# All modulation rows summed in the first stage, and expert value sums on four tiles of the TensorE array

## The chip, the cores and the metric

The kernel runs on one core of a Trainium2 chip. It is one launch that computes two networks one after the other, in float32. The metric is the device time of a launch in microseconds (us); less is better.

## The reference, cut to what matters

The first network has two layers over 256 rows of `x` and 256 rows of `ctx`, 1024 wide. Each layer begins from modulation rows, one matrix product of two vectors with a large weight:

```python
mod_x = silu(c) @ ada_w[i] + ada_b[i]        # 1024 x 6144 weights per layer
mod_c = silu(c_ctx) @ ada_w[i] + ada_b[i]
sh1, sc1, g1, sh2, sc2, g2 = split(mod_x, 6)
xn = rmsnorm(x, norm1_g[i]) * (1 + sc1) + sh1
x = x + g1 * mixer(xn)                       # layer 0: chunk mixer, layer 1: state-space mixer
x = x + g2 * peer(rmsnorm(x, norm2_g[i]) * (1 + sc2) + sh2)
```

`peer` picks, for each token and each of 8 heads, 16 of 16384 experts, and needs a row `u` and a row `v` of each:

```python
ue, ve = take(u_tab, ids), take(v_tab, ids)              # 1024 wide each
act = gelu(einsum("nd,nhkd->nhk", h, ue))
y = einsum("nhk,nhkd->nd", g * act, ve)
```

`ctx` goes through the same in layer 0, and in layer 1 only gives the state-space mixer its starting state. The second network (attention, latent attention, two feed-forwards) follows and is not touched.

## The kernel before

**Stages.** The front (0 to about 310 us) makes the modulation rows of layer 0, the chunk mixer of `ctx`, and the matrices of the state-space mixer. The first expert stage, `peer0` (about 304 to 1828 us), sums experts for 256 `ctx` tokens and then 256 `x` tokens; in its gaps run, as "fill", the chunk mixer of `x`, the modulation rows of group 0 of layer 1 (`ada1`), and the state-space input, states and scan of `ctx`. Then comes the state-space mixer of `x` (about 1828 to 2060), the second expert stage `peer1` (about 2100 to 2786), and the second network.

**Modulation rows.** A layer's weight is 24 blocks of 1 MB, in three groups of 8: group 0 holds shift and scale of the first norm, group 1 the mixer's gate and the second norm's shift, group 2 that norm's scale and the expert gate. `Rows` (L465) does one group: `load(j)` puts a block in a slot of `W`, after the slot's last user (`w_used`); `pe` sums it with 64 matmuls of 64 columns whose outputs lie on four column tiles of the array (L495); `add_bias` (L504) takes the sums and adds the bias on DVE; `store` (L513) sends four small DMAs from ACT's queue to `mod_scr`, from which the norms load them. The front holds the three groups of layer 0, two blocks between two blocks of the mixer's input product (`pe_in`, L627). `ada1` sits in the fill of `peer0`, at `ADA1_ROW`. The last two groups of layer 1 are `LateRows` (L1636 to 1664): 16 blocks loaded by POOL, pair by pair, into buffers that the first expert stage has left, and summed between the pieces of the state-space mixer of `x`.

**Expert stage.** For each of 512 or 256 (block of tokens, head, choice) triples, a "row": POOL gathers for 128 tokens the row of `u` and of `v` (1 MB, L1350) into a ring of 8; DVE multiplies with `h` and sums (L1326); ACT does gelu, the gate, and scales the identity to a 128 x 128 diagonal `DIAG` (L1218, L1220, L1223); PE multiplies the diagonal with the two halves of `v` into two banks (L1165), accumulating over 16 rows, a "unit". After a unit `add_rows` on DVE multiplies both banks by the gate (L1307, 1024 columns at once) and adds to `XA` (L1308), at the tenth row of the next unit. Between rows PE does the queries of later heads (L1126) and one step of fill. Steps of the fill are placed by row numbers.

**State-space mixer of x.** Eight chunks; each is cut by ACT from `u_scr`, turned (L1444), summed with a 1 MB matrix of `min_scr` (L1690), turned again (L1708), and copied by ACT and DVE (L1501, L1522). DVE then scans 31 steps for the first half of the groups (`dve_scan(0)`, four chunk copies inside it) and 31 for the second half; output products (L1828, L1830) follow each half, then the projection (L1873).

**Order.** Each engine's instructions are in program order, as are the DMAs of a queue. SP issues nearly all weight loads; ACT issues the stores of matrices and rows, so a slow issue there holds up its copies. The orders of the front are written out in `first_sync`, `first_pe`, `first_act`, `first_dve`, `first_pool`.

Of the kernel before, what the change touches and what calls it, by code (L numbers as in the profile page):

```python
# [15 lines left out]
ALU = mybir.AluOpType  # L16
# [9 lines left out]
P = 128  # L26
D = 1024
KT = D // P
# [76 lines left out]
def program(nc, t):  # L105
    with ExitStack() as ctx:
# [361 lines left out]
        class Rows:  # L468
# [3 lines left out]
            def __init__(self, layer, grp, slots, bank, bias, stage, saved):  # L472
                self.layer, self.grp, self.slots, self.bank = layer, grp, slots, bank
                self.bias, self.stage, self.saved = bias, stage, saved
                self.slot_of = [slots[j % len(slots)] for j in range(8)]
                self.n = [use(s) for s in self.slot_of]
                self.kept, self.stored = saved.plan(1), mod_stored.plan(64)
                bias_in.plan(16)
# [4 lines left out]
            def load_bias(self, eng):  # L483
                eng.dma_start(self.bias, t["ada_b"][self.layer * 3 + self.grp].rearrange("p (a e) -> p a e", a=2)).then_inc(bias_in.sem, 16)

            def pe(self, row0=0, per=1, blocks=range(8)):
                for j in blocks:
                    s = self.slot_of[j]
                    if j == 0:
                        pe.wait_ge(self.saved.sem, self.kept if self.saved is sums_taken else self.kept - 1)  # L490
# [10 lines left out]
            def add_bias(self):  # L501
                v.wait_ge(bias_in.sem, 64 if self.layer else 48)
# [89 lines left out]
        class Mixer:  # L592
# [60 lines left out]
            def pe_mix(self):  # L653
                yield from until("pe", self.mix_row)
                pe.wait_ge(w_full[3], (self.n_ws + 1) * 16)
                for j in range(2):
                    pe.wait_ge(v_done.sem, self.vv + j + 1)
# [377 lines left out]
        class Peer:  # L1035
# [10 lines left out]
            DIAG = view(20224, 4, P)  # L1046
# [98 lines left out]
            def pe(self, fill, after_first=None):  # L1145
# [7 lines left out]
                for r in range(self.rows):  # L1153
# [46 lines left out]
            def act(self, fill, after_first=None, tail=iter(())):  # L1200
# [9 lines left out]
                for u in range(self.units):  # L1210
                    a.wait_ge(gate_ready.sem, self.gr + u + 1)
                    for k in range(TOPK):
# [10 lines left out]
                        a.mul(self.DIAG[:, r % 4, :], IDENT, self.WGT[:, u % 2, k:k + 1]).then_inc(diag_ready.sem, 1)  # L1223
# [75 lines left out]
            def add_rows(self, u):  # L1299
# [6 lines left out]
                sums = PS[:, 4 + (u % 2) * 2:6 + (u % 2) * 2, :].rearrange("p a b -> p (a b)")  # L1306
                dve.link(v, v.tensor_tensor(self.YG, sums, gate, ALU.mult))  # L1307
# [5 lines left out]
            def dve(self, fill, tail=iter(())):  # L1313
                for u in range(2):
                    drain(self.choose(u))
                self.gates(0)
# [298 lines left out]
        STAGE2 = [AR[0:ADA_LANES, at:at + 512] for at in (23680, 24192)]  # L1615
# [4 lines left out]
        ROW_IN = [XA[:, 2:4, :].rearrange("p t d -> p (t d)"), H[:, 2:4, :].rearrange("p t d -> p (t d)"), view(14464, BLK), view(16512, BLK)]  # L1620
        BIAS2 = [HT[0:ADA_LANES, 2 * i:2 * i + 2, SEQ:SEQ + COLS] for i in range(2)]


        row_in, row_used, row_added = [sem(f"ada2_in{u}") for u in range(2)], sem("ada2_used"), sem("ada2_added")
        row_out, bias2_in = [sem(f"ada2_out{u}") for u in range(2)], sem("ada2_bias_in")

        class LateRows:


            BANK, PAIRS = 6, 8  # L1630

            def load(self, p):
                for j in (2 * p, 2 * p + 1):
                    if j >= 4:
                        g.wait_ge(row_used, p - 1)
                    g.dma_start(ROW_IN[j % 4], t["ada_w"][32 + j]).then_inc(row_in[p % 2], 16)  # L1636

            def load_bias(self):
                for grp in range(2):
                    sp.dma_start(BIAS2[grp], t["ada_b"][4 + grp].rearrange("p (a e) -> p a e", a=2)).then_inc(bias2_in, 16)  # L1640

            def pe(self, p):
                if p == 0:
# [1660 lines left out]
```

## Time and profile before

| | us |
|---|---|
| median of three runs | 3702.83 (3699.62 to 3703.74) |
| the profiled execution, time | 3701.66 |
| its span, first to last instruction | 3699.7 |
| PE, DVE, ACT, POOL busy | 3170.0, 2248.0, 1430.1, 969.0 |
| moved by DMA | 1152.69 MB, mean 312 GB/s |

Line numbers are those of the kernel before. A recorded float32 matmul is two instructions, so the two matmuls of a row show as x4. The profiled execution's time lies 1.17 us under the median, and 1.96 us of it lies outside the span.

### The profile page before, as it was taken

Reading aid. Unit: us, or ns where it says so; the run is one execution under the profiler, and the core shown is the slowest. Engines: PE = TensorE matmul, PEld = TensorE weight load, DVE = VectorE, ACT = ScalarE, POOL = GpSimd, SP = SyncE. Lnnn points to the kernel's source line nnn. Section 1 sums busy time; section 2 is a strip of 40 time slices with the busy share of each in tenths; the row PEclk is TensorE's granted clock in tenths of the full one; section 3 lists DMA queues with packets and bytes.
Section 4 is the critical chain, followed back from the end, with each engine's and each line's share of the span. In section 5 each row is a group of like instructions: output and inputs, shape, how many; then the busy total and the mean of one; then the engine's idle time right before and its main releaser. Section 6 shows DMA issues by size and latency. Waiting matters only on the chain. (4 is left out here: it accounts for less than half of the span.)

```text
span 3699.7 us, 46712 instructions
## 1 busy us (share of the span) xinstructions
PE 3170.0 (86%) x15952; PEld 2093.8 (57%) x15952; DVE 2248.0 (61%) x5034; ACT 1430.1 (39%) x3564; POOL 969.0 (26%) x796
## 2 busy tenths in 40 slices
PE   4977999899888998897767798888877989889898
PEld 3865566454434654442356644444325789777897
DVE  6855667666667666679424467666762259513397
ACT  1223443444334444443223244444432247423275
POOL 0002434434333334444200154444560000000000
PEclk8977999999999999999877899999998989999899
DMA  7748999999999999999876499999992325332353
GB/s 278 289 169 320 420 415 413 421 419 417 420 420 395 411 407 415 414 419 348 364 274 214 174 421 421 421 421 416 414 418 108 120 104 181 136 117 105 120 183 119
DMA packets 177137, 1152.69 MB, mean 312 GB/s; under 512 B 21860, under 2 KB 30264, under 8 KB 43306
## 3 DMA queue, kind: packets, MB, share of 16 engines
q0 software_dynamic: 113936, 827.38, 54.6%
q1 hardware_dynamic: 56058, 304.90, 21.9%
q10 hardware_dynamic: 6944, 17.91, 1.3%
q8 instruction: 105, 1.72, 0.2%
q14 instruction: 94, 0.77, 0.1%
HBM read 1128.86 MB, written 21.25 MB: 311 GB/s over the span
## 5 line engine op out<-in xcount | busy, mean ns | idle before, releaser
L1165 PE MATMUL PS<-AR 128*128 128x512 f32 x3072 | 1510.2, 618 | 252.0 <-ACT AR L1223 245.7
L1350 POOL DMA_INDIRECT AR<-in_peer_uv,AR x768 | 955.8, 1245 | 1503.5 <-PE PS L1165 1095.2
L1326 DVE CUSTOM_DVE_ANT_0 AR<-AR,H 128x1024 f32<-128x1024 f32 x768 | 940.7, 1225 | 655.8 <-DMA AR<-in_peer_uv,AR 637.0
L1165 PEld LDWEIGHTS PS<-AR 128*128 128x128 f32 x3072 | 558.8, 193 | 856.9 <-issue 419.0
L1218 ACT ACTIVATE SM<-SM 128x1 f32<-128x1 f32 x768 | 155.3, 202 | 1130.4 <-DVE SM L1326 1126.1
L1126 PEld LDWEIGHTS PS<-HT,W 128*128 128x128 f32 x1536 | 299.7, 195 | 271.0 <-issue 254.6
L1126 PE MATMUL PS<-HT,W 128*128 128x256 f32 x1536 | 428.1, 387 | 2.0 <-issue 1.3
L1223 ACT ACTIVATE AR<-CON,SM 128x128 f32<-128x128 f32 x768 | 308.4, 402 | 48.1 <-PE PS L1165 23.7
L2623 PE MATMUL PS<-XP,WP 128*128 128x256 f32 x2112 | 265.2, 288 | 13.2 <-ACT WP L2769 7.0
L2623 PEld LDWEIGHTS PS<-XP,WP 128*128 128x128 f32 x2112 | 264.0, 197 | 15.6 <-issue 7.3
L1220 ACT ACTIVATE SM<-SM 128x1 f32<-128x1 f32 x768 | 226.3, 295 | 25.0
L627 PE MATMUL PS<-W,HT 128*128 128x256 f32 x768 | 192.8, 391 | 5.8 <-ACT AR L724 2.8
L627 PEld LDWEIGHTS PS<-W,HT 128*128 128x128 f32 x768 | 149.5, 197 | 37.7 <-issue 16.2
L2769 ACT CAST WP<-AR 128x2048 fp32r<-128x2048 f32 x66 | 126.5, 1917 | 49.9 <-DVE AR L2612 49.9
L2815 DVE TENSOR_TENSOR WP<-W,AR 128x2048 fp32r<-128x2048 f32 x62 | 142.1, 2292 | 2.1
L2623 PE MATMUL PS<-WP,GVP 128*128 128x512 f32 x528 | 128.0, 399 | 11.8 <-DVE GVP L2618 11.8
L2623 PEld LDWEIGHTS PS<-WP,GVP 128*128 128x128 f32 x528 | 100.6, 194 | 33.1 <-issue 12.6
L2612 DVE TENSOR_SCALAR AR<-W 128x2048 uint32<-128x2048 uint32 x62 | 75.8, 1223 | 18.8 <-PE PS L2623 15.6
L495 PE MATMUL PS<-W,SM 128*2 128x64 f32 x2048 | 48.8, 241 | 36.3 <-DMA W<-in_ada_w 33.3
L495 PEld LDWEIGHTS PS<-W,SM 128*2 128x2 f32 x2048 | 34.1, 93 | 61.4 <-issue 36.2
L1242 DVE MAX8 SM<-AR 128x8 f32<-128x128 f32 x96 | 23.2, 283 | 71.3 <-ACT AR L1192 40.8
L2974 PE MATMUL PS<-HT,W 128*128 128x256 f32 x288 | 65.0, 388 | 0.5 <-ACT HT L262 0.5
(374 smaller groups left out, 3414.1 us busy)
## 6 DMA issues: line engine op xcount, KB each, us to landing
W<-in_peer_w_q SPq DMA_DIRECT2D x48, 1024.0 KB
W<-in_ada_w SPq DMA_DIRECT2D x32, 1024.0 KB
W<-in_ffn_out SPq DMA_DIRECT2D x22, 1024.0 KB
W<-in_ffn_gate SPq DMA_DIRECT2D x20, 1024.0 KB
W<-in_ffn_val SPq DMA_DIRECT2D x20, 1024.0 KB
W<-in_cm_w_in SPq DMA_DIRECT2D x16, 1024.0 KB
AR<-min_scr SPq DMA_DIRECT2D x16, 1024.0 KB, 10.3
AR<-in_peer_uv,AR POOLq DMA_INDIRECT x768
```

The costliest lines, as they stand in the source:

```text
L495: mm = pe.matmul(PS[32 * c:32 * c + 2, self.bank, j * ADA_PART:(j + 1) * ADA_PART], CS[:, k, :], W[:, s, at:at + ADA_PART], start=(k == 0) ...
L627: mm = pe.matmul(self.bank(i)[:, j * COLS:(j + 1) * COLS], HT[:, k, tb * P:(tb + 1) * P], W[:, slot, k * COLS:(k + 1) * COLS], start=(k == ...
L1126: mm = pe.matmul(PS[:, j % 2, 0:2 * P], W[:, j // 2, k * COLS + (j % 2) * P:k * COLS + (j % 2 + 1) * P], HT[:, k, first:first + 2 * P], st ...
L1165: mm = pe.matmul(PS[:, 4 + (u % 2) * 2 + c, :], self.DIAG[:, r % 4, :], self.UV[:, r % RING, D + c * 512:D + (c + 1) * 512], start=(k == 0 ...
L1218: a.activation(self.GELU[:, u % 2, one], self.ACTV[:, u % 2, one], ACT.Gelu_apprx_tanh).then_inc(gelu_done.sem, 1)
L1220: a.mul(self.WGT[:, u % 2, one], self.GELU[:, u % 2, one], self.GATE[:, u % 2, one]).then_inc(w_ready.sem, 1)
L1223: a.mul(self.DIAG[:, r % 4, :], IDENT, self.WGT[:, u % 2, k:k + 1]).then_inc(diag_ready.sem, 1)
L1326: v.tensor_tensor_reduce(rows_, rows_, H[:, self.tb(u), :], 1.0, 0.0, ALU.mult, ALU.add, self.ACTV[:, u % 2, k:k + 1]).then_inc(u_used.sem, 1)
L1350: g.indirect_dma_start(out=self.UV[:, r % RING, :], out_offset=None, in_=t["peer_uv"], in_offset=bass.IndirectOffsetOnAxis(ap=self.IDS[:, ...
L2623: mm = pe.matmul(out, lhs[i], rhs[j], start=(start and n == 0), stop=(stop and n == 2))
L2769: a.copy(WP[:, s, 0, :], WT).then_inc(high_done, 1)
L2815: v.tensor_tensor(WP[:, s, 1, :], src, WT, ALU.subtract).then_inc(split_done, 1)
```

## The change

It has two parts.

**Rows.** `ada` is now six `Rows`, all in the front; `ada1`, `LateRows` and their semaphores, waits, loads and stores are gone. The second group of layer 0 is summed whole before the mixer's first block; groups 2 and 3 go between the eight blocks of `pe_in`, one pair after each; groups 4 and 5 go, pair by pair, between the two halves of `pe_mix`, after `pe_turn`, after the sixth and the seventh piece of the matrices, and after each of the four blocks of `pe_out`. All of them use slots 0 and 1. `add_bias` and `store` of each follow on DVE and ACT. SP's load order is rewritten to match, and the peer stage's own first loads stand behind the last row block. The load of `x` now waits for all six groups (`mod_stored` 384 in place of 192).

**Value sums.** A row's two matmuls (128 x 128 diagonal, 512 columns) become four, each on a 64 x 64 tile: token half `half` is the row half of the array and picks the bank, column half `c` of `v` is the column half. The diagonal is 128 x 64 (`EYES`, two stacked 64 x 64 identities, made once per expert stage). `add_rows` takes the sums in four pieces of 64 partitions x 512 columns in place of one of 128 x 1024.

```diff
+                self.n_th, self.layer, self.grp, self.bank, self.saved = n, n // 3, n % 3, 6 + n % 2, ada_saved
+                self.slots = slots = (0, 1) if n else (0, 1, 2, 3)
 ...
-                    for c in range(2):
-                        mm = pe.matmul(PS[:, 4 + (u % 2) * 2 + c, :], self.DIAG[:, r % 4, :], self.UV[:, r % RING, D + c * 512:D + (c + 1) * 512],
-                                       start=(k == 0), stop=(k == TOPK - 1))
+                    for x in range(2):
+                        for half in range(2):
+                            c, rows_ = (half + x) % 2, slice(half * self.HP, (half + 1) * self.HP)
+                            mm = pe.matmul(PS[c * self.HP:(c + 1) * self.HP, 4 + (u % 2) * 2 + half, :], self.DIAG[rows_, r % 4, :],
+                                           self.UV[rows_, r % RING, D + c * 512:D + (c + 1) * 512], start=(k == 0), stop=(k == TOPK - 1))
 ...
-                        a.mul(self.DIAG[:, r % 4, :], IDENT, self.WGT[:, u % 2, k:k + 1]).then_inc(diag_ready.sem, 1)
+                        a.mul(self.DIAG[:, r % 4, :], self.EYES, self.WGT[:, u % 2, k:k + 1]).then_inc(diag_ready.sem, 1)
 ...
-                sums = PS[:, 4 + (u % 2) * 2:6 + (u % 2) * 2, :].rearrange("p a b -> p (a b)")
-                dve.link(v, v.tensor_tensor(self.YG, sums, gate, ALU.mult))
+                for i in range(2):
+                    for c in range(2):
+                        out, here, cols = slice(i * self.HP, (i + 1) * self.HP), slice(c * self.HP, (c + 1) * self.HP), slice(c * 512, (c + 1) * 512)
+                        one = v.tensor_tensor(self.YG[out, cols], PS[here, 4 + (u % 2) * 2 + i, :], gate[here, cols], ALU.mult)
+                dve.link(v, one)
 ...
-            for b in range(4):
+            mixc.load_out(0)
+            for one in ada[4:6]:
+                one.load_bias(sp)
+            for b in range(6):
+                ada[4].load(b)
+            for b in range(1, 4):
                 mixc.load_out(b)
+                for at in (2 * b + 4, 2 * b + 5):
+                    ada[4 + at // 8].load(at % 8)
+            for b in range(4, 8):
+                ada[5].load(b)
             peer0.sync(fill_sync())
 ...
             for b in range(8):
                 drain(mixc.pe_in(b))
-                if b < 7:
-                    at = (2 * b + 2) % 8
-                    drain(ada0[1 if b < 3 else 2].pe(blocks=range(at, at + 2)))
+                at = 2 * b % 8
+                drain(ada[2 + b // 4].pe(blocks=range(at, at + 2)))
                 if b in (1, 2, 4, 5, 7):
                     prep.pe((1, 2, 4, 5, 7).index(b))
-            drain(mixc.pe_mix())
+            drain(mixc.pe_mix(lambda: drain(ada[4].pe(blocks=range(0, 2)))))
             drain(mixc.pe_turn())
+            drain(ada[4].pe(blocks=range(2, 4)))
             prep.pe(5)
+            drain(ada[4].pe(blocks=range(4, 6)))
             for b in range(4):
                 drain(mixc.pe_out(b))
+                at = (2 * b + 6) % 8
+                drain(ada[4 if b == 0 else 5].pe(blocks=range(at, at + 2)))
             prep.pe(6)
+            drain(ada[5].pe(blocks=range(6, 8)))
             drain(norm2c.pe())
```

Taken out beside these: `late.pe`, `late.load`, `late.add_bias` and `late.store` at all their places, SP's waits for them (`row_used`, `row_out`), and `ada1`'s load, sums, bias and store in the fill.

## Rows read from the trace of the kernel before

**Rows 1.** Busy time by stretch: engines, PE clock, DMA share, GB/s.
```profile
200.00:250.00 50.00, 42.28 (x228) 38.22 (x227) 40.44 (x53) 12.52 (x20) 1.56 (x3) 0.91 0.54 203
400.00:800.00 400.00, 383.04 (x1282) 231.04 (x1281) 264.45 (x621) 169.10 (x493) 159.87 (x134) 1.00 1.01 417
2400.00:2650.00 250.00, 219.94 (x596) 106.38 (x594) 174.03 (x420) 106.54 (x321) 119.42 (x96) 0.99 1.01 419
```
**Rows 2.** Order of time on PE in the front; in brackets idle before, and releaser.
```profile
66.40 1.94 PE L585 MATMUL PS<-CON,H 128*128 128x128 f32 x8 [14.79 <-issue]
134.43 1.07 PE L495 MATMUL PS<-W,SM 128*2 128x64 f32 x64 [1.39 <-DMA W<-in_ada_w]
169.76 1.97 PE L495 MATMUL PS<-W,SM 128*2 128x64 f32 x128
180.81 1.09 PE L886 MATMUL PS<-CON,AR 128*128 128x128 f32 x8 [1.10 <-ACT AR L858]
195.25 3.75 PE L663 MATMUL PS<-AR,W 128*128 128x128 f32 x16 [7.99 <-ACT AR L716]
208.34 27.87 PE L627 MATMUL PS<-W,HT 128*128 128x256 f32 x128
243.26 1.97 PE L886 MATMUL PS<-CON,AR 128*128 128x128 f32 x8 [6.17 <-ACT AR L858]
```
**Rows 3.** Order of time on ACT, end of the front.
```profile
253.93 5.79 ACTq L875 DMA_DIRECT2D lag_scr<-H  x8
259.75 1.07 ACT L555 COPY HT<-PS 128x512 f32<-128x512 f32 x2 [7.45 <-DMA mout_scr<-AR]
```
**Rows 4.** DMA issues and totals, 870 to 1060 us, where `ada1` runs.
```profile
DMA packets 11230, 79.68 MB, mean 419 GB/s; under 512 B 1246, under 2 KB 1246, under 8 KB 1600
W<-in_ada_w SPq DMA_DIRECT2D x8, 1024.0 KB
```
**Rows 5.** Order of time in pure expert rows: PE's value sums, DVE's taking.
```profile
2761.17 1.98 PE L1165 MATMUL PS<-AR 128*128 128x512 f32 x4 [0.50 <-ACT AR L1223]
2785.53 1.22 DVE L1307 TENSOR_TENSOR AR<-PS,AR 128x1024 f32<-128x1024 f32 x1 [3.07 <-PE PS L1165]
```
**Rows 6.** Order of time on PE, sums on tiles: four column tiles, then two row tiles.
```profile
1903.13 1.04 PE L1690 MATMUL PS<-AR 128*32 128x256 f32 x16
2846.84 0.70 PE L2457 MATMUL PS<-AR 64*128 64x256 f32 x4
2847.48 0.70 PE L2459 MATMUL PS<-AR 128*128 128x256 f32 x2
```
**Rows 7.** Order of time on PE: a long wait in the first expert stage.
```profile
1112.61 3.78 PE L1165 MATMUL PS<-AR 128*128 128x512 f32 x4 [7.72 <-ACT AR L1223]
```
**Rows 8.** Busy time by 20 us, columns as in rows 1: end of the `ctx` scan.
```profile
1660.00:1680.00 20.00, 14.45 (x24) 4.75 (x22) 18.99 (x50) 5.24 (x18) 5.63 (x6) 0.83 0.93 376
1720.00:1740.00 20.00, 16.11 (x28) 5.99 (x29) 19.04 (x51) 9.87 (x28) 8.07 (x6) 0.83 0.80 290
```
**Rows 9.** Order of time on PE in the state-space mixer of `x`.
```profile
1899.81 1.89 PE L1650 MATMUL PS<-XA,SM 128*2 128x64 f32 x64 [5.59 <-DMA H<-in_ada_w]
```
**Rows 10.** Order of time on DVE there: chunk copies, scans, the late bias.
```profile
1889.43 1.06 DVE L1522 COPY AR<-PS 64x256 f32<-64x256 f32 x2 [51.76 <-PE PS L1708]
1893.66 1.02 DVE L1522 COPY AR<-PS 64x256 f32<-64x256 f32 x2 [3.17 <-PE PS L1708]
1917.17 0.19 DVE L1794 COPY AR<-AR 128x64 f32<-128x64 f32 x1
1952.93 0.69 DVE L1657 TENSOR_TENSOR AR<-PS,HT 98x512 f32<-98x512 f32 x1
```
**Rows 11.** DVE's waits 1917 to 1953 us: total, times, longest, in us.
```profile
DVE AR L1522 <- PE PS L1708: 7.0, 3, 3.9
```
**Rows 12.** DMA issues 1860 to 1925 us: count, size, median us to landing.
```profile
AR<-in_ada_w POOLq DMA_DIRECT2D x6, 1024.0 KB, 10.9
AR<-min_scr SPq DMA_DIRECT2D x5, 1024.0 KB, 13.2
```

More of the change, by code:

```diff
@@ L651, in pe_in, with pe_mix @@
                 yield from self.block(b, 2 + b % 2, self.n_in[b], self.row0 + b * 2 * KT / self.IN, self.IN)
-            def pe_mix(self):
+            def pe_mix(self, between=None):
                 yield from until("pe", self.mix_row)
@@ L656, in pe_mix @@
                 for j in range(2):
+                    if j and between:
+                        between()
                     pe.wait_ge(v_done.sem, self.vv + j + 1)
@@ L1315, in dve @@
                     drain(self.choose(u))
+                for i in range(2):
+                    half = slice(i * self.HP, (i + 1) * self.HP)
+                    dve.link(v, v.tensor_copy(self.EYES[half], IDENT[half, half]))
                 self.gates(0)
@@ L1983, in fill_sync @@
             sp.dma_start(G2X, row(mod_scr[0, 0, 5 * D:6 * D])).then_inc(g2_in.sem, 16)
-            yield from until("sp", ADA1_ROW - 6)
+            yield from until("sp", normc.row0 - 4)
             sp.wait_ge(n_h.sem, norm2x.h_at)
-            ada1.load_bias(sp)
-            for j in range(8):
-                yield from until("sp", ADA1_ROW + (j - 1) * KT / ADA1_RATE - 4)
-                ada1.load(j)
-            yield from until("sp", normc.row0 - 4)
-            sp.wait_ge(mod_stored.sem, 256)
             normc.load(sp)
@@ L2035, in fill_act @@
             yield from norm2x.turned()
-            yield from until("act", ADA1_ROW + 8 * KT / ADA1_RATE + 3)
-            ada1.store()
             yield from normc.stats()
@@ L2077, in first_sync @@
             for j in range(4):
-                ada0[0].load(j)
-            for one in ada0:
+                ada[0].load(j)
+            for one in ada[0:4]:
                 one.load_bias(sp)
@@ L2129, in first_sync @@
                 outs.load_lags(c)
-            for u in range(2):
-                sp.wait_ge(row_out[u], 64)
             sp.wait_ge(y_sums, NCH)
@@ L2140, in first_pe @@
             pe.wait_ge(cond_done, 1)
-            drain(ada0[0].pe())
-            drain(ada0[1].pe(blocks=range(2)))
+            drain(ada[0].pe())
+            drain(ada[1].pe())
             pe.wait_ge(con_in, 16)
@@ L2213, in first_act @@
             mixc.act_sums()
-            ada0[1].store()
+            ada[2].store()
             mixc.act_squares()
@@ L2223, in first_act @@
             matrices(4)
-            ada0[2].store()
+            ada[3].store()
             drain(mixc.act_mix())
@@ L2229, in first_act @@
                 drain(mixc.act_out(b))
+                if b == 2:
+                    ada[4].store()
             drain(norm2c.stats())
@@ L2233, in first_act @@
             drain(norm2c.turned())
+            ada[5].store()
             def rest_of_matrices():
@@ L2260, in first_act @@
                     statex.act_forward(c - 1)
-                if c == 3:
-                    late.store(0)
                 if c > NCH // 2:
@@ L2265, in first_act @@
             outs.act_save(0)
-            late.store(1)
             for c in range(1, NCH):
@@ L2361, in first_pool @@
             peer0.pool()
-            g.wait_ge(lag_out, 16)
-            late.load(0)
-            g.wait_ge(x_ready.sem, x1_ready + 2)
-            for p in range(1, late.PAIRS):
-                late.load(p)
             peer1.pool()
```

109 lines of the change are left out of this document (35 added, 74 removed).

## The prediction

> **What bounds the kernel now.** I read the busy time by stretch first, since every stage has its own limit. In the expert stages the DMA share is 1.01 at 417 to 419 GB/s [rows 1]: with that, a faster engine gains nothing and a megabyte less gains its transfer time. PE is nearly as busy in the first expert stage (383.04 of 400 us), so the two limits are close there; in the second it is busy 219.94 of 250. The front is different: DMA share 0.54 at 203 GB/s, PE busy 42.28 of 50 us [rows 1], so it is bound by PE and by the copies between its steps, and DMA has room. Then I read PE's and ACT's order of time in the front, and PE's, DVE's and the DMA issues in the state-space mixer of `x`. There the sums of late rows wait for their own loads [rows 9], the 1 MB matrices of the chunks take 13.2 us to land beside late loads of 10.9 us [rows 12], and DVE's scan, which ends the chain, waits for chunks [rows 11].
>
> **Part 1a, 24 row blocks into the front.** A pair of blocks costs PE 1.97 us at full clock [rows 2]. The front held 24 blocks and now holds 48: 12 pairs more.
> - Three pairs (group 1, blocks 2 to 7) now stand ahead of the mixer. Between the blocks that they replace and the first norm PE idles 14.79 us [rows 2], waiting for DVE's powers, and 6 MB at 419 GB/s are 15.0 us. I take them as hidden; they free the places of three pairs between the mixer blocks. If the norm's own load of 1.5 MB gets half the DMA engines it takes 7 us and just makes it; otherwise 1 to 3 us are lost.
> - So the eight places between mixer blocks hold 8 pairs in place of 7: +1.97 us. One more bias load on SP, ahead of the matrices' parameters: +0.7 us, estimated from SP's issues.
> - One pair inside `pe_mix` falls in an idle time of 7.99 us in which ACT is issuing stores [rows 2]: 0, and up to 2 if its load comes late.
> - Two pairs around the sixth piece of the matrices: +3.9 us.
> - Pairs after the four output blocks: the first three lie ahead of the last block, +5.9 us, and each now waits for 3 MB (a pair and an output block, 7.5 us at 419 GB/s, plus a landing time) while PE works only 27.87 / 4 = 7.0 us on a block [rows 2]. In the input part of the front the same arrangement without a piece of matrices between costs a wait of 1.39 us [rows 2]. I take 1.4 each for two of them, and 2.3 for the first, which meets the store of a 1 MB matrix and the norm's rows: +5.1 us.
> - The fourth pair falls in the 6.17 us wait for ACT [rows 2]: 0. That wait gets shorter, and behind it PE ran at half clock (1.97 us for what takes 1.09 at full clock [rows 2]): -2 us, between 0 and -4.
> - The last pair lies beside ACT's issue of stores, 5.79 us, during which ACT's copies wait 7.45 us [rows 3]: 0. The biases and stores on DVE and ACT (0.69 and some 1.3 us each) lie in waits of those engines.
>
> Sum: 0.7 + 2.0 + 3.9 + 5.9 + 5.1 - 2 = **+15.6 us**, between +9 (no DMA waits, full clock gain) and +25 (each of the seven pairs behind the mixer input waits 2 us more). The expert stage's first weights now stand behind the last row load on SP; they have about 8 us before the queries need them, which 2 MB need 5 us of.
>
> **Part 1b, group 0 of layer 1 out of the first expert stage.** It is 8 loads of 1 MB in a stretch with 79.68 MB at 419 GB/s [rows 4]. The DMA share is full, so the stage shortens by their transfer: 8 x 1.049 MB + 0.2 MB of bias, 8.59 MB / 419 GB/s = **-20.5 us**. PE's 8 us for them go too, hidden. If PE were the limit instead, the gain would be those 8 us: that is the bound from above; -22 from below.
>
> **Part 1c, 16 late blocks out of the state-space mixer.** DVE's first scan begins at 1917.17, behind the copy of the fourth chunk [rows 10]. The first two chunks were copied at 1889.43 and 1893.66, 4.2 us apart; from there on PE waits for late loads, 5.59 us at the first [rows 9]. Without them two more chunks at 4.2 us end at 1902 + 1 us of copy = 1903. Two late pairs that lay on PE's path ahead of the second chunk go too, 1.97 us each and somewhat more with what they wait for, 5 us in sum: 1898, a shift of -19. A chunk's matrix is loaded when the one two before it is summed; 1 MB needs 2.5 us and its landing time, so a step of 4.2 is possible. Within the scan DVE waits three times for chunks, 7.0 us in sum [rows 11]; chunks at 4.2 us run ahead of the scan, which takes one every seventh step (36 us less 7, over 4: 7 us), so this goes: -7. The late bias goes: -0.7 [rows 10]. The second scan and all behind it follow at once. Sum: **-27 us**. From below -31, if the read of `u_scr` also lands earlier; from above -18, if the matrices' loads pace the chunks at 6 us and the scan still waits.
>
> **Part 2, value sums on four tiles.** A row costs PE 1.98 us now, with 0.50 us idle ahead: 2.48 us, which is 1 MB at 421 GB/s [rows 5]. After the change a row is 8 recorded instructions of 512 columns, 0.49 us each if alone. Four column tiles run 16 instructions of 256 columns in 1.04 us [rows 6], where 16 in a row cost 27.87 / 128 = 0.218 each [rows 2], 3.5 us: a factor of 3.3. Taking that for 2 x 2 tiles, 8 x 0.49 / 3.3 = 1.2 us a row. The bounds are 0.98 (all four at once) and 3.9 (one after another, like none of the rows). But rows arrive every 2.5 us or more, so nearly all of this gain is idle time.
> - Where PE and DMA are both full, DMA falls short of its best for moments: 417 against 421 GB/s over 1240 us is 12 us at most, part of it small packets. I take -2, between 0 and -7.
> - DVE takes a unit in four pieces; a piece of 512 columns is 0.69 us long [rows 10], I take 0.62 from start to start, so 2.5 us against the 1.25 of L1307 [rows 5]: +1.25 per unit, 48 units, 60 us in all. It is hidden where DMA is full, since DVE is busy 174.03 of 250 us [rows 1]. It is not where DVE is full: the four stretches from 1660 to 1740, the first at 18.99 and the last at 19.04 of 20 us with the DMA share down to 0.80 [rows 8]. They hold 27 gathers, 1.7 units: +2.1. And the stats of the next norm wait in ACT for the taking of the last `ctx` unit, which stops PE for 7.72 us [rows 7]: +1.3. At the end of the second expert stage the take is on the path [rows 5], +1.25, less 0.8 for the value sums and 0.1 for a smaller diagonal: +0.3.
>
> Sum: -2 + 2.1 + 1.3 + 0.3 = **+1.7 us**, between -5 and +5.
>
> A rule that speaks against this part: two row tiles of 64 follow and precede full 128 x 128 matmuls in the attention, and the pair takes 0.64 us from its start to the next one's [rows 6], where 4 instructions at 0.218 with both tiles at once would take 0.44. The Trainium skill, TensorEngine Tiling (Array Packing), Key Properties, says that changing the tiling mode, not just the tile, drains TensorE; the trace agrees, at about 0.1 us a change. With it the sum doesn't move, since the row then costs 1.4 us; it returns below as a rival.
>
> **Sum.** 15.6 - 20.5 - 27 + 1.7 = -30.2 us. Against the profiled execution's own 3701.66 that is 3671.5; it lay 1.17 us under the median of the runs, which gives 3672.6. I say **3672**.
>
> **The rivals.**
> - *A, the front gives back most of it.* The load path (slots 0 and 1 alone, one queue, in order) can't keep up beside stores and the norm's rows, and each of the last seven pairs waits 3 us more than taken: +21, so 3693. For it: seven blocks of 2 and 3 MB stand behind one another on SP. Against: DMA is at 203 GB/s there [rows 1], and 16 MB more in some 65 us are 250 GB/s more, 450 in all: over what it can do, by the sum itself. That makes it serious; the front then takes 4 us more from bytes alone, which my +5.1 covers.
> - *B, a larger gain.* The front's pairs hide better (+9), PE's relief gives -7, the state-space part -31: -50, 3653.
> - *C, slower: value sums become the bound.* Where queries and fill lie between the value sums, PE changes between 64 x 64 and full tiles two to four times in a row. A row of the first stage takes 400 us / 134 = 2.98 us [rows 1]; queries and fill take about 1.35 of it (383.04 / 134 = 2.86, less 1.5 for value sums not hidden by overlap). The change costs time once value sums and switches together pass 1.6 us; at 3.9 us (tiles one after another) a row would take 5.2 us, 2.2 more for some 480 rows and 1.4 more for the rest, over 1400 us. Nearer the point, at 1.9 us, it is 0.3 x 420 rows = 125 us, 3798. Against it stand the factor 3.3 of the column tiles and the two row tiles at 0.64 us [rows 6]. The drain of the rule above is how it would come about: at 0.1 us a change it doesn't, at 0.2 and four changes it would.
> - *D, no change.* The state-space part gains only -12, because the next loads in line (output matrices, lags, weights) fill the freed DMA time, and the front costs +22: 15.6 and 27 become 22 and 12, the sum -9 to -3, 3697.
>
> **Chances.** Forecast, between -18 and -42: 0.62. A: 0.14. B: 0.11. C: 0.05. D: 0.08. A difference of under 0.2% (7.4 us) is about what a measurement of this kernel can't tell from none. Forecast, A and B are faster; D is half within, some slower. Faster 0.88, same 0.06, slower 0.06. The range takes in the forecast's bounds and most of A and B: 3648 to 3692.
>
> **What would show it.** The first gather would be issued 15 us later than before; if 26 or more, part 1a is wrong. DMA stays at full share through the first expert stage, which is shorter by about 19 us from first gather to last; if by more than 25, PE was the limit. From the last value sum of that stage to the projection's first matmul 172 us become about 145, with DVE's scan unbroken. L1165 shows 8 instructions a row in 1.0 to 1.5 us, and the idle ahead of it grows to over 1 us. If row time rises above 2.5 us in the second expert stage, part 2 is wrong in sign.

## The result, and the profile after

The changed kernel took 3683.46 us at the median against 3702.83, a ratio of 0.9941 with a 95% interval of 0.9927 to 0.9955: 19.4 us less. In a second set of runs the same kernel gave 0.9954 (0.9939 to 0.9969), 15.4 us less. The profiled execution took 3687.25 us with a span of 3685.4, so its span lies 14.3 us under that of before; both profiled executions of the changed kernel were the slowest of their sets, 3.8 and 4.0 us over the median. The forecast was 30 us. I first cut both spans at the same five events, each read from the order of time of its engine, and added the kernels of the experiments.

| | first gather | from it to the last value sum of the first expert stage | to the projection | to the next gather | to the last take of a unit | to the end |
|---|---|---|---|---|---|---|
| before | 303.68 | 1523.7 | 170.0 | 102.3 | 687.1 | 912.9 |
| after | 341.53 | 1503.7 | 140.6 | 102.1 | 688.0 | 909.4 |
| after, second set (after_again) | 339.49 | 1504.4 | 141.7 | 103.1 | 687.4 | 913.2 |
| rows_only | 339.49 | 1503.1 | 141.3 | 100.9 | 687.3 | 909.7 |
| tiles_only | 301.47 | 1522.3 | 171.7 | 102.2 | 688.3 | 908.2 |
| sums_no_loads | 322.33 | 1500.8 | 138.4 | 101.9 | 687.5 | 909.6 |
| loads_no_sums | 334.96 | 1504.4 | 138.5 | 99.9 | 688.3 | 908.5 |
| half_loads | 335.81 | 1502.7 | 141.0 | 101.6 | 687.3 | 909.4 |
| three_slots | 340.50 | 1505.1 | 137.9 | 100.0 | 687.3 | 910.2 |
| group1_between | 366.14 | 1506.3 | 140.1 | 99.9 | 687.6 | 909.8 |
| stores_later | 336.33 | 1502.8 | 140.2 | 101.9 | 687.6 | 910.0 |
| slots_and_stores | 333.22 | 1503.4 | 139.4 | 101.9 | 688.5 | 908.5 |
| late_no_loads | 304.32 | 1525.1 | 152.9 | 101.8 | 686.8 | 909.3 |
| sums_twice | 338.86 | 1556.1 | 137.3 | 99.6 | 689.3 | 910.6 |

(us; the first column counts from the start, the others from the event before.) The first gather is the start of the first expert stage. The change gives 20.0 us in the first expert stage and 29.4 in the state-space mixer, and the front takes 37.9 back. The last column is the second network, which no kernel here touches. It scatters from 908.2 to 913.2 between executions, so 3.5 of the 14.3 us of this pair of spans are no effect of the change, and a front difference under 2 us isn't one either. The columns of the state-space mixer (137.3 to 141.7 us) and of what follows it (99.6 to 103.1) also scatter between kernels that are the same there.

**Front.** PE's waits after the change, between 60 us and the first gather (engine, line, releaser: sum, times, longest):

```profile
PE PS L499 <- DMA W<-in_ada_w: 24.8, 15, 5.9
PE PS L894 <- ACT AR L866: 11.8, 8, 4.1
PE PS L591 <- ACT HT L561: 6.3, 1, 6.3
PE PS L671 <- ACT AR L724: 4.0, 1, 4.0
```

L499 is the rows' sums, L894 the matrices, L591 the norm's product, L671 the mix; L633, below, is the mixer's input and output blocks. The first of these waits was 2.5 us before. The order of time on PE after the change (start, us, line, operation; in brackets the idle time before and its releaser), which answers to [rows 2]:

```profile
65.93 1.89 PE L499 MATMUL PS<-W,SM 128*2 128x64 f32 x64 [5.88 <-DMA W<-in_ada_w]
68.39 1.88 PE L499 MATMUL PS<-W,SM 128*2 128x64 f32 x64 [0.58 <-DMA W<-in_ada_w]
72.88 1.89 PE L499 MATMUL PS<-W,SM 128*2 128x64 f32 x64 [2.60 <-DMA W<-in_ada_w]
76.70 1.89 PE L499 MATMUL PS<-W,SM 128*2 128x64 f32 x64 [1.93 <-DMA W<-in_ada_w]
78.52 3.82 PE L591 MATMUL PS<-CON,H 128*128 128x128 f32 x16
83.01 7.17 PE L633 MATMUL PS<-W,HT 128*128 128x256 f32 x32 [0.67 <-ACT HT L561]
...
207.82 1.28 PE L499 MATMUL PS<-W,SM 128*2 128x64 f32 x64 [2.22 <-DMA W<-in_ada_w]
213.14 3.75 PE L671 MATMUL PS<-AR,W 128*128 128x128 f32 x16 [4.04 <-ACT AR L724]
...
233.95 1.89 PE L499 MATMUL PS<-W,SM 128*2 128x64 f32 x64 [2.76 <-DMA W<-in_ada_w]
```

Three pairs were to hide in the 14.79 us idle ahead of the first norm [rows 2]. They don't: the last blocks of the group arrive at 66 to 77 us, the norm's product starts at 78.52 in place of 66.40, and the mixer's first block at 83.01 in place of 71.65. The busy time in that very idle time, and in the 12.1 us behind it, says why (from:to, length, then busy PE, PEld, DVE, ACT, POOL, PE clock, DMA share, GB/s); before:

```profile
51.60:66.40 14.80, 0.01 (x1) 0.03 (x1) 13.63 (x44) 0.00 (x0) 1.00 (x2) 0.50 0.57 204
66.40:78.50 12.10, 10.76 (x36) 8.66 (x37) 11.88 (x14) 3.62 (x5) 0.00 (x0) 0.56 0.16 66
```

and after:

```profile
51.60:66.40 14.80, 5.21 (x182) 4.35 (x174) 12.12 (x47) 0.00 (x0) 1.05 (x2) 0.50 0.96 354
66.40:78.50 12.10, 6.99 (x248) 5.92 (x236) 4.92 (x5) 0.00 (x0) 0.00 (x0) 0.50 0.68 252
```

PE was idle there, but DMA was not: it moved 204 GB/s, 3.0 MB, already. At 419 GB/s that leaves room for 3.2 MB of the six blocks' 6.3, and the rest is 7 us of transfer (an estimate from these rows). An engine's idle time is cover for its own work only; the loads needed idle time of DMA.

**Expert stages.** The stretches of [rows 1] after the change:

```profile
400.00:800.00 400.00, 329.49 (x1808) 150.99 (x1808) 278.92 (x661) 164.44 (x498) 150.68 (x136) 0.95 1.01 420
2400.00:2650.00 250.00, 176.91 (x962) 54.24 (x962) 184.95 (x440) 99.07 (x317) 102.27 (x96) 0.88 1.01 418
```

PE is busy 54 us less of 400 and 43 less of 250, and DMA moves 420 and 418 GB/s where it moved 417 and 419. The value sums after, which answer to [rows 5], at the end of the first stage and, with the take, at the end of the second:

```profile
1840.89 1.09 PE L1176 MATMUL PS<-AR 64*64 64x512 f32 x8 [1.40 <-ACT AR L1234]
1843.35 1.86 PE L1176 MATMUL PS<-AR 64*64 64x512 f32 x8 [1.37 <-ACT AR L1234]
...
2773.19 2.79 DVE L1320 TENSOR_TENSOR AR<-PS,AR 64x512 f32<-64x512 f32 x4 [2.15 <-PE PS L1176]
```

A row is 1.09 us at full clock and the idle time ahead grew from 0.50 to 1.4: what PE gains becomes idle time. The take costs 2.79 us.

**State-space mixer.** DVE around the start of the scan, which answers to [rows 10]:

```profile
1904.45 1.02 DVE L1539 COPY AR<-PS 64x256 f32<-64x256 f32 x2 [3.34 <-PE PS L1679]
1907.49 1.02 DVE L1539 COPY AR<-PS 64x256 f32<-64x256 f32 x2 [2.02 <-PE PS L1679]
1910.56 1.02 DVE L1539 COPY AR<-PS 64x256 f32<-64x256 f32 x2 [2.05 <-PE PS L1679]
1911.98 0.20 DVE L1764 COPY AR<-AR 128x64 f32<-128x64 f32 x1 [0.40 <-ACT AR L1518]
```

The chunks follow one another every 3.1 us. From the last value sum to the scan it is 66.8 us where it was 89.8.

### The profile page after: what moved, and what is told of

Read it like the earlier page. It is cut to its first block and busy times, and to the rows that moved or that the text cites. A ratio compares the mean times of both kernels' runs of the same rounds, so it can differ in the third digit from the quotient of the medians.

```text
span 3685.4 us, 53007 instructions
## 1 busy us (share of the span) xinstructions
PE 2839.4 (77%) x19024; PEld 1690.9 (46%) x19024; DVE 2319.5 (63%) x5182; ACT 1388.9 (38%) x3564; POOL 851.5 (23%) x780
## 5 line engine op out<-in xcount | busy, mean ns | idle before, releaser
L1176 PE MATMUL PS<-AR 64*64 64x512 f32 x6144 | 985.6, 722 | 550.1 <-ACT AR L1234 548.7
L1367 POOL DMA_INDIRECT AR<-in_peer_uv,AR x768 | 846.9, 1103 | 1686.0 <-PE PS L1176 1176.8
L1176 PEld LDWEIGHTS PS<-AR 64*64 64x64 f32 x6144 | 181.8, 148 | 1000.3 <-ACT AR L1234 878.6
L1135 PE MATMUL PS<-HT,W 128*128 128x256 f32 x1536 | 501.6, 436 | 2.1 <-issue 1.4
L1135 PEld LDWEIGHTS PS<-HT,W 128*128 128x128 f32 x1536 | 264.4, 200 | 478.0 <-issue 460.6
L1234 ACT ACTIVATE AR<-AR,SM 128x64 f32<-128x64 f32 x768 | 267.1, 348 | 25.3 <-PE PS L1176 0.2
L633 PE MATMUL PS<-W,HT 128*128 128x256 f32 x768 | 203.5, 406 | 16.1 <-ACT AR L698 12.8
L633 PEld LDWEIGHTS PS<-W,HT 128*128 128x128 f32 x768 | 152.1, 203 | 60.8 <-issue 37.7
L2730 ACT CAST WP<-AR 128x2048 fp32r<-128x2048 f32 x66 | 126.5, 1917 | 49.9 <-DVE AR L2573 49.9
L1320 DVE TENSOR_TENSOR AR<-PS,AR 64x512 f32<-64x512 f32 x192 | 132.2, 688 | 5.7 <-PE PS L1176 2.2
L499 PE MATMUL PS<-W,SM 128*2 128x64 f32 x3072 | 63.5, 249 | 64.9 <-DMA W<-in_ada_w 61.4
L499 PEld LDWEIGHTS PS<-W,SM 128*2 128x2 f32 x3072 | 54.6, 97 | 75.0 <-DMA W<-in_ada_w 54.3
L2935 PE MATMUL PS<-HT,W 128*128 128x256 f32 x288 | 65.3, 389 | 0.5 <-ACT HT L262 0.5
```

The source lines that it names most:

```text
L633: mm = pe.matmul(self.bank(i)[:, j * COLS:(j + 1) * COLS], HT[:, k, tb * P:(tb + 1) * P], W[:, slot, k * COLS:(k + 1) * COLS], start=(k == ...
L1135: mm = pe.matmul(PS[:, j % 2, 0:2 * P], W[:, j // 2, k * COLS + (j % 2) * P:k * COLS + (j % 2 + 1) * P], HT[:, k, first:first + 2 * P], st ...
L1176: mm = pe.matmul(PS[c * self.HP:(c + 1) * self.HP, 4 + (u % 2) * 2 + half, :], self.DIAG[rows_, r % 4, :], self.UV[rows_, r % RING, D + c ...
L1234: a.mul(self.DIAG[:, r % 4, :], self.EYES, self.WGT[:, u % 2, k:k + 1]).then_inc(diag_ready.sem, 1)
L1320: one = v.tensor_tensor(self.YG[out, cols], PS[here, 4 + (u % 2) * 2 + i, :], gate[here, cols], ALU.mult)
L1367: g.indirect_dma_start(out=self.UV[:, r % RING, :], out_offset=None, in_=t["peer_uv"], in_offset=bass.IndirectOffsetOnAxis(ap=self.IDS[:, ...
```

## The experiments

**Each part alone.** `rows_only` takes the value sums back to two matmuls; `tiles_only` is the kernel before with the four tiles:

```diff
-                    for x in range(2):
-                        for half in range(2):
-                            c, rows_ = (half + x) % 2, slice(half * self.HP, (half + 1) * self.HP)
+                    for c in range(2):
+                        mm = pe.matmul(PS[:, 4 + (u % 2) * 2 + c, :], self.DIAG[:, r % 4, :], ...
```

> The changed kernel with the value sums of before (a 128 x 128 diagonal, two matmuls a row, one take of 1024 columns): the rows are moved, nothing else. Theory R (all of the gain is the moved rows, the tiles bring nothing): 19 to 22 us under the kernel before, first gather 38 us later than before, 20 us shorter from the first gather to the last value sum of the first expert stage. Rival T (part of the gain is PE's relief by the tiles): only 8 to 14 us under, and the first expert stage shorter by 10 to 15 us. Rival C (the take in four pieces costs): 25 us or more under.

> The kernel before with the value sums on four tiles: the rows stay where they were. Theory R: within 3 us of the kernel before (forecast on record for this part +1.7, bounds -5 and +5); a row's sums take 1.1 us at full clock. Rival T: 5 to 10 us under it, by a shorter first expert stage. Rival C: 4 us or more over it.

`rows_only`: 0.9935 (0.9921 to 0.9948), 23.6 us under, a little over theory R's 19 to 22; front, first stage and state-space mixer as in the changed kernel within 2.1 us. `tiles_only`: 0.9999 (0.9990 to 1.0008), 0.3 us under. Its stages are those of before within 2.2 us, and DMA's share stays 1.01 at 420 GB/s:

```profile
400.00:800.00 400.00, 335.26 (x1836) 156.19 (x1832) 276.60 (x655) 163.25 (x495) 147.95 (x135) 0.95 1.01 420
```

Theory R holds by the stages: the gain is the moved rows, and rival T falls. Rival C is not shown and not ruled out: the intervals of `rows_only` and of the changed kernel overlap, and no stage ahead of the second network differs by more than 2.2 us. The second set of the changed kernel was to tell: 16 to 21 us under the kernel before, so it was written ahead of the run, if the tiles cost something beside the moved rows, 21 to 26 if the difference was scatter. It came 15.4 us under. That leans to a small cost, but the two kernels ran in different sets, and their intervals overlap here too.

**How far PE is from the limit.** `sums_twice` makes each row's tile sums twice (`for again in range(2)` around them).

> The changed kernel, but each row's four tile sums are made twice into the same banks, so the expert sums are twice those of the reference (other experts may be chosen behind that). A row then has 2.2 us of value sums at full clock, and twice as much at half clock. By the bound written for rival C (time is lost once value sums and tile changes pass 1.6 us a row), 0.6 us on some 420 rows, 250 us, are lost. Theory K (that bound was too low: the kernel before had 1.98 us a row and was held by DMA): the first expert stage longer by 0 to 20 us, the second not at all.

The first expert stage grew by 52 us, the second by 1.3; ratio 1.0089 (1.0072 to 1.0106). PE's order of time in the first stage:

```profile
604.85 1.95 PE L1177 MATMUL PS<-AR 64*64 64x512 f32 x16
606.73 0.70 PE L1135 MATMUL PS<-HT,W 128*128 128x256 f32 x2
607.27 1.03 PE L633 MATMUL PS<-W,HT 128*128 128x256 f32 x4
608.22 1.95 PE L1177 MATMUL PS<-AR 64*64 64x512 f32 x16
```

A stretch of that stage with much fill, by busy time, in the kernel with the sums made twice:

```profile
500.00:600.00 100.00, 98.44 (x655) 45.07 (x647) 58.42 (x143) 35.82 (x113) 33.10 (x29) 1.00 0.94 361
```

and in the kernel before:

```profile
500.00:600.00 100.00, 100.00 (x338) 62.74 (x337) 62.12 (x150) 46.16 (x131) 39.56 (x34) 1.00 1.01 414
```

A row takes 3.37 us there without idle time, so PE is the limit, and DMA falls to 361 GB/s. The kernel before, with 1.98 us of value sums and no change between tile sizes, stood just at that point: PE without idle time, DMA still at 414. Sixteen tile instructions take 1.95 us, about the same, and the changes between 64 x 64 and full tiles come on top. `rows_only`, with 1.98 us a row and no such changes, took 1503.1 us for this stage, so the changes are the likely price of the 52 us; no run takes them out by themselves. Neither theory had it: the loss is a fifth of the 250 us, and over twice the 20.

**What the front pays for: transfers or sums.** In `sums_no_loads` SP counts the slot as full without loading; in `loads_no_sums` PE makes one matmul in 64. In `half_loads` half of each block is loaded.

The first, the second and the third edit:

```diff
+                if self.layer:
+                    sp.wait_ge(w_used[self.slot_of[j]], self.n[j] + 1)
+                    sp.sem_inc(w_full[self.slot_of[j]], 16)
+                    return
 ...
+                        if self.layer and k < KT - 1:
+                            continue
-                        for c in range(4):
+                        for c in range(3 if self.layer else 0, 4):
 ...
+                part = BLK // 2 if self.layer else BLK
+                load(self.slot_of[j], self.n[j], t["ada_w"][...][:, 0:part], part)
```

> The changed kernel, but the 24 row blocks of layer 1 are not loaded: PE sums what lies in the slots, so the modulation rows of layer 1 are not those of the reference. PE's work in the front stays, 25 MB of transfers go. Theory W (in the second half of the front the sums wait for their loads and slow the other transfers): the first gather goes from 341.5 to 327 to 331 us, the time to some 12 us under the changed kernel. Rival P (PE's own time for the pairs is the cost, the waits only fill what would be idle): first gather 338 or later, time within 4 us of the changed kernel.

> The changed kernel, but of the 64 matmuls of each row block of layer 1 only the last is made, so the modulation rows of layer 1 are not those of the reference. All transfers stay, 12 pairs of 1.97 us of PE time go. Theory W: most of the time saved on PE comes back as waits for the next load: the first gather 328 to 333 us. Rival P: the pairs' own time goes in full, first gather 316 to 322 us.

> The changed kernel, but of each row block of layer 1 only the first half is loaded (512 KB in place of 1 MB); PE still makes all 64 matmuls, half of them on what was in the slot before, so the rows of layer 1 are not those of the reference. Theory Y (bytes: the transfers of the second half of the front share 16 engines, and 25 MB less brought the first gather from 341 to 322): half the bytes give half of it, first gather 329 to 333. Rival N (the number of loads in two slots, each with its time from issue to landing, sets it): first gather 336 or later.

Without the transfers the first gather comes at 322.3, 17 to 19 us earlier, more than theory W's 10 to 14. The mixer still starts at 82.6 there, since the three pairs ahead of it belong to layer 0, so these 17 to 19 us come on top of the 11.4 ahead of the mixer. Without the sums it comes at 335.0, 4.5 to 6.6 earlier, later than W's 328 to 333, and that for 24 us of PE time. So rival P falls: the sums cost little, the transfers do not. The medians are 35.3 us under the kernel before without the transfers (0.9917, 0.9902 to 0.9932), 28.3 without the sums (0.9926, 0.9910 to 0.9941) and 27.8 with half loads (0.9923, 0.9907 to 0.9940), where the changed kernel has 19.4 and 15.4; by these the sums may cost more than the one trace shows. PE's waits from 83 us to the first gather, with half of each block loaded:

```profile
PE PS L895 <- ACT AR L867: 11.8, 8, 4.1
PE PS L672 <- ACT AR L725: 7.5, 1, 7.5
PE PS L592 <- ACT HT L562: 5.5, 1, 5.5
PE PS L500 <- DMA W<-in_ada_w: 2.1, 2, 1.4
```

The waits for row loads, 13.8 us in the changed kernel past the mixer's start, shrink to 2.1, but part of it moves to ACT's copies (7.5 us at the second half of the mix, 4.0 in the changed kernel). The second norm's last product starts at 292.5, 7 to 9 us earlier than in the changed kernel (301.4 and 299.4), where no transfers give 283.8: half the bytes, about half the gain, as theory Y has it. At the first gather itself it was 335.8, between the two theories' numbers, since the queries behind the norm ran slower in this execution (43.3 us from that product to the gather; 40.2 and 40.1 in the changed kernel, 38.6 without transfers). Y is likely by the first reading, not settled by the second.

**The group ahead of the mixer.** `three_slots` loads it into slots 0, 1 and 3 in turn, and the load of the mixer's second block moves behind it, since slot 3 was that block's; `group1_between` puts three of its pairs back between mixer blocks:

```diff
-                self.slots = slots = (0, 1) if n else (0, 1, 2, 3)
+                self.slots = slots = ((0, 1, 2, 3), (0, 1, 3))[n] if n < 2 else (0, 1)
 ...
-            drain(ada[1].pe())
+            drain(ada[1].pe(blocks=range(2)))
 ...
-                drain(ada[2 + b // 4].pe(blocks=range(at, at + 2)))
+                for _ in range(2 if b < 3 else 1):
+                    one, at = next(in_order)
+                    drain(ada[one].pe(blocks=range(at, at + 2)))
```

> The changed kernel, but the second group of layer 0, which stands ahead of the mixer, is loaded into three slots in turn (0, 1, 3) in place of two; the mixer's second block comes behind it. Theory S (each block's load is started only when the slot's last block is summed, 8 us from issue to landing, two at a time: the 11.4 us that the mixer starts later than before are latency): mixer starts at 77 to 80 in place of 83.0, first gather 3 to 6 us earlier. Rival B (the DMA engines are full up to there, so bytes set it): mixer starts at 82 to 84, no gain.

> The changed kernel, but three pairs of the second group of layer 0 go back between the mixer's blocks, so that the first three gaps hold two pairs each and nothing but what was there before stands ahead of the first norm. Theory S: the mixer starts at 72 again, but the gaps with two pairs wait for their loads (5 MB a block against 11 us of PE), so the input part takes some 12 us more: the first gather within 4 us of 341.5. Rival F (6 MB ahead of the norm was simply the wrong place): the input part takes 6 us more at most, the first gather 5 to 9 us earlier than in the changed kernel.

With three slots the mixer starts at 77.77, as theory S has it. So some 5 of the 11.4 us go with two slots in turn; up to 2.5 of them (an estimate: 1 MB at 419 GB/s) may be the mixer block that moved. The other 6 stay, with DMA now at a share of 1.01 and 409 GB/s from 51.6 to 66.4 us: those are bytes, as rival B had it for all of them. But the first gather comes at 340.5, no earlier than in the second execution of the changed kernel, and the ratio is the same, 0.9951 (0.9938 to 0.9965). Where those 5 us go, the runs don't settle; PE's matrices and mixer blocks ran at half clock for longer (4.2 us more busy time in sum than in the first execution of the changed kernel).

`group1_between` is slower than the kernel before: 1.0024 (1.0011 to 1.0037), first gather at 366.1. Both theories missed it. PE there:

```profile
73.13 8.57 PE L633 MATMUL PS<-W,HT 128*128 128x256 f32 x32 [0.68 <-ACT HT L561]
81.64 1.97 PE L499 MATMUL PS<-W,SM 128*2 128x64 f32 x128
87.93 1.89 PE L499 MATMUL PS<-W,SM 128*2 128x64 f32 x64 [4.33 <-DMA W<-in_ada_w]
91.04 1.89 PE L499 MATMUL PS<-W,SM 128*2 128x64 f32 x64 [1.22 <-DMA W<-in_ada_w]
92.86 8.95 PE L633 MATMUL PS<-W,HT 128*128 128x256 f32 x32
```

The second pair of a gap can be asked for only when the first has been summed, so each such gap waits a whole landing (4.3, 4.0 and 6.1 us), PE's clock falls, and the next mixer block's load stands behind those loads on SP. The group ahead of the mixer costs 11 us and is still the cheaper place.

**ACT's issue of stores.** `stores_later` moves the stores of the fifth and seventh piece behind the copies that the mixer and the norm wait for:

```diff
-            matrices(4)
-            ada[3].store()
+            matrices(4, False)
             drain(mixc.act_mix())
             drain(mixc.act_turn())
-            matrices(5)
+            prep.act_store(4)
+            ada[3].store()
             for b in range(4):
                 drain(mixc.act_out(b))
+                if b == 0:
+                    matrices(5)
 ...
-            matrices(6)
+            matrices(6, False)
             drain(norm2c.turned())
+            prep.act_store(6)
             ada[5].store()
```

> The changed kernel, but ACT issues the stores of the fifth and the seventh piece of the matrices behind the copies that the mixer and the second norm wait for, and not ahead of them; the sixth piece goes behind the first output block. Theory I (in these two places ACT's issue of stores, 10.9 us ahead of the mix copies and 6 us ahead of the norm's, is what PE waits for, in the changed kernel as in the kernel before): first gather 8 to 14 us earlier than 341.5 and the time 8 to 14 us under the changed kernel. Rival L (the rows' loads set the pace of that part of the front): first gather at most 4 us earlier, since the waits for in_ada_w grow by what ACT's go down.

> The changed kernel with both rearrangements of the front that gave something: three slots for the second group of layer 0, and ACT's issue of stores behind the copies in two places. If they add up: first gather 334 to 336, time 4 to 8 us under the changed kernel. If the transfers behind them take back what the earlier start of the mixer gives (as with three slots alone, 5 us at the mixer and 1 at the first gather): first gather 336 to 339.

ACT's order of time in the changed kernel, where those stores hold up the mix copies:

```profile
202.94 8.14 ACTq L883 DMA_DIRECT2D lag_scr<-H  x8
211.17 1.20 ACTq L519 DMA_DIRECT2D mod_scr<-XA  x4
212.41 1.07 ACT L724 COPY AR<-PS 128x512 f32<-128x512 f32 x2 [10.94 <-DMA mout_scr<-AR]
```

With the stores later the second half of the mix starts at 204.71 (213.14, and 209.25 in the second execution), and the norm's second product follows the first after 1.4 us and not 7.4. Yet the first gather is only 3 to 5 us earlier, at 336.3, near rival L's "at most 4". PE in `stores_later`, with the sixth piece (L902) and the first queries (L1137) behind the waits for rows:

```profile
211.71 7.17 PE L633 MATMUL PS<-W,HT 128*128 128x256 f32 x32
222.23 1.65 PE L499 MATMUL PS<-W,SM 128*2 128x64 f32 x64 [3.35 <-DMA W<-in_ada_w]
227.56 1.89 PE L499 MATMUL PS<-W,SM 128*2 128x64 f32 x64 [3.68 <-DMA W<-in_ada_w]
234.22 6.87 PE L902 MATMUL PS<-AR 128*128 128x32 f32 x32
295.75 7.14 PE L1137 MATMUL PS<-HT,W 128*128 128x256 f32 x32 [2.20 <-DMA W<-in_peer_w_q]
```

But L's reason, that the waits for `in_ada_w` grow, is not what the trace shows: behind the mixer's start they are 12.0 us in sum, where they were 13.8 and 14.8. What grew is PE's own time at the lower clock: the matrices take 60.1 us of it where they took 52.8 and 53.5, the sixth piece 6.87 us for what took 3.66. And PE now waits 2.2 us for the queries' weight and 2.4 for ACT behind the norm. The ratio, 0.9943 (0.9926 to 0.9959), can't be told from that of the changed kernel. With three slots as well the first gather is at 333.2, 6 to 8 us earlier, and all stages up to the end of the second expert stage take 2766.4 us where the changed kernel took 2776.0 and 2776.2. Its ratio, 0.9944 (0.9930 to 0.9958), 24.3 us under the kernel before by medians, beats that kernel; that it beats the changed one is suggested by its one trace and not shown. The gather came 1 to 3 us earlier than the 334 to 336 written for the case that the two parts add up.

**The late rows' loads.** `late_no_loads` is the kernel before with POOL counting up in place of 16 loads (`g.sem_inc(row_in[p % 2], 16)`).

> The kernel before, but the 16 late row blocks are not loaded; PE sums what lies in their buffers at the same places, so the late rows are not those of the reference. From the last value sum of the first expert stage to the projection it took 170 us before and takes 141 in the changed kernel. Theory D (as forecast: of the change there, some 5 us are PE's own time for the pairs, the rest is transfers): 144 to 150 us, and the time 20 to 26 under the kernel before. Rival E (PE's 8 pairs of 1.97 us lie on the path in full): 155 us or more, 15 under at most.

The part from value sums to projection took 152.9 us, between the two. Of the 29 us, 17 are the loads, and 11 to 12 are what is left: the sums, their biases and the waits that come with them, among them one of 4.9 us on PE ahead of the fourth chunk for which the profile names no releaser. That is more than the 5 I gave PE. By the median it is 20.6 us under the kernel before, which is in theory D's 20 to 26. Ratio 0.9954 (0.9936 to 0.9971).

## Why the prediction was right, and where it was wrong

**The total is in part luck.** 3683.46 us is 11.5 over the forecast of 3672 and 9.5 under rival A's 3693. It lies in the range because the range took in most of A. Of the forecast's own band, 18 to 42 us less, the first set reached the near end (19.4) and the second missed it (15.4). And by the sign that I wrote down, a first gather 26 us or more later, part 1a is wrong: it came 37.9 us later.

**Right in sign, and in three of four terms.** First expert stage: forecast -20.5, measured -20.0 (and -20.6 with the rows alone), from bytes over bandwidth. State-space mixer: -27, measured -29.4. Its parts: scan start -19, measured -23.0; waits inside the scan and the late bias -7.7, measured -6.7 (29.7 us where it was 36.4); the chunks' step 4.2, measured 3.1, the likely reason why it gave more. The split of the -19 into PE and loads was off: with the loads alone gone (`late_no_loads`) the scan starts 79.1 us after the last value sum, so 10.7 of the 23.0 are the loads and 12.3 the rest, for which I had 5. Part 2: +1.7, measured -0.3 by itself, within what can be told. Its mechanism holds: row 1.09 us (forecast 1.2), idle time ahead 1.4; the take 2.79 us (forecast 2.5).

**Wrong in one term: the front, +15.6 forecast, +37.9 and +35.8 measured**, over its upper bound of 25. By steps:
- "Three pairs ... I take them as hidden": 0 forecast, 11.4 measured. This is the step that failed. It weighed 6 MB against the 14.79 us in which PE was idle as if DMA were free there, and DMA had a share of 0.57 at 204 GB/s: room for about half. "Otherwise 1 to 3 us are lost" had no row behind it. Of the 11.4, some 5 go with the two slots in turn.
- From the mixer's start to the mix, the eighth pair and the bias load: 2.7, measured 4.3. The pair itself is 1.9; of the rest 1.5 is the first piece of the matrices, 8.2 us where it took 6.6.
- The pair inside the mix: 0 to 2, measured 2.2. It did fall into the idle time, but ACT's issue of the small stores, which ends that idle time, took 8.14 us and not 6.04.
- The two pairs around the sixth piece: 3.9, measured 9.5: 3.3 us of waits for loads (0.54 and 2.76), and half clock behind them (1.89 for a block that takes 1.07 at full clock).
- Pairs after the output blocks: 11.0, measured 12.1. Behind them -2 was forecast and -1.7 measured.

So half of the 22.3 us by which the front was over lies ahead of the mixer, and most of the rest at the mix and behind it.

The front's sum is near rival A, which held that the load path can't keep up and the front takes 21 us more than forecast: 36.6, and 37.9 came. That is partly chance too. A put all 21 us into waits of the last seven pairs, 26 with the 5.1 that the forecast had, and these pairs wait 10.7 us for their loads in the changed kernel; 11.4 of the excess are ahead of the mixer, where A had nothing. What the runs bear out of A is its kind of reason: the transfers on two slots cost 17 to 19 us behind the mixer's start, the sums 5 to 7. I gave it 0.14 because DMA's mean share of 0.54 in one stretch [rows 1] looked like room; I had even worked out 450 GB/s of demand in the same sentence, over anything that the rows show. That a stretch of 50 us has room on the mean says little where two slots bound what can be asked for ahead.

**Rival C** named a point, 1.6 us a row, from which value sums cost time. The rows speak against it: the kernel before spent 1.98 us [rows 5], and DMA was full at 417 GB/s in the first expert stage [rows 1]. The runs put the point near 2 us, and the price of passing it by the tile changes at some 52 us, not the 125 worked out for 0.3 us a row.

**The change of tile size.** Two query instructions between value sums took 0.43 us from start to start before and take 0.63 with the tiles; eight tile instructions take 1.02 us to the next start and sixteen 1.88, so 0.16 beyond the 0.86 for eight. That is 0.36 us a row for two changes, nearer 0.2 each than the 0.1 that I took, and it cost nothing here, since PE has the time. The Trainium skill, TensorEngine Tiling (Array Packing), Key Properties, states that a changed tiling mode drains TensorE; the trace agrees, at some 0.2 us a change.

## What to carry to other kernels

Before moving work with its loads into an engine's idle time, read DMA's share in that very window, and how many loads the free slots let be under way: by the first gather the sums of 24 blocks cost 5 to 7 us in the front, their 25 MB 17 to 19. Bytes taken out of a stretch with full DMA share gave their transfer time (20.0 and 20.6 us, 20.5 forecast), and a faster PE operation there gave nothing, while PE still had idle time. Cutting all kernels at the same events shows where a change acts, and the same stage in kernels that leave it alone shows how much of it is scatter, here up to 5 us.

## What the runs showed of the hardware

- Eight instructions of 64 x 64 tiles and 512 columns take 1.09 us and sixteen 1.95, so 0.86 for eight more. The same sums on the full array took 1.98 us, and some 1.71 from start to start where a query followed at once. That is 1.8 times as fast for eight alone and 2.0 in a run of them.
- Shorter value sums lowered the clock: the mean granted clock of the profiled execution was 0.941 for the kernels with the value sums of before (0.944 for `late_no_loads`) and 0.867 to 0.879 for those with four tiles, and 0.941 again with the sums made twice. In the second expert stage it went from 0.99 to 0.88, and a row made after more idle time took 1.86 us at the lower level. `tiles_only` shows that it cost no time in sum.
- The issue of eight small stores on ACT isn't a fixed price: 3.9 to 8.4 us over the runs. Ahead of the mix it took 6.04 us before, 8.14 and 7.90 in the changed kernel, 7.32 with half loads and 6.67 without the loads of layer 1. But the next eight went from 6.13 to 4.02 us, and the last ones ahead of the norm from 5.79 to 8.35, also without those loads (8.34), so what sets it stays open.
